# The last two expert blocks' rows enter the residual by one-hot gate products on TensorE, and the reload of the scattered rows waits for the third block from the end

## The chip, the cores and the metric

The kernel runs on one NeuronCore of a Trainium2 chip. The metric is the device time of one execution in microseconds, as a median of runs. The core has five instruction streams: PE (TensorE, matrix products), DVE (VectorE), ACT (ScalarE), POOL (GpSimd) and SP (SyncE, which issues DMAs here). They run in their own order and meet only at semaphores.

## The reference, cut to what matters

Two layers of a decoder trunk. Each is a token mixer (RWKV-7, then MoBA attention), a cross-attention and a mixture of experts; only the last matters here. 512 tokens of 1024 channels are routed to 2 of 32 experts each:

```
    y = lax.map(expert_block, (x_rows, block_expert)).reshape(n_rows, C)
    out = jnp.zeros((N, C), F32).at[row_tok].add(y.astype(F32) * row_gate[:, None])
    ...
        x = x + hierarchical_moe(h2, moe_wg[i], moe_bg[i], moe_we[i], moe_be[i],
                                 moe_w1[i], moe_w3[i], moe_w2[i]).reshape(B, T, C)
    return rms_norm(x, ln_f)
```

So each token gets two expert rows, each times its gate, added to the residual `x`. After layer 0 `x` is normed and multiplied by the query weights of MoBA (`mq`); after layer 1 it is normed and written out.

## The kernel before, in words

**Expert blocks.** The token rows are grouped into blocks of 64 rows, one expert a block, and 32 blocks ran in each layer of this execution (`E` is 32; blocks beyond `E` exist in the program behind branches, as an overflow). POOL gathers the 64 rows of a block from `h_rows` in HBM; PE turns them (`rows_in`), multiplies them by the two up matrices (`up`), turns the gated result (`turn_act`) and multiplies by the down matrix (`down`). DVE makes the gated product (`gated`), ACT copies the 128x512 result out of PSUM into `y[b]`, of which there are two, and POOL scatters it to `y_rows` in HBM by `scatter`, an indirect DMA. SP streams the expert matrices.

**The combine.** When the last block's rows have landed in `y_rows`, SP loads them back token by token: 8 DMAs of 512 KB (`combined[t]`, t = 0 to 3 tiles of 128 tokens, k = 0 and 1 the two experts of a token), in the order of t. DVE adds each, times its gate, to `x[:, t]` (`combine(t, k)`, line 1969). Then for each tile ACT takes the squares (line 857), DVE and ACT make the reciprocal root (lines 1235, 859, 1237), and DVE scales: line 1994 for layer 0, whose result PE turns (line 2413) and multiplies by the `mq` weights (line 2426), or `finished` at line 1984 for layer 1, after which SP stores the tile.

**Other loads of SP at this place.** In layer 0 the first pair of `mq` matrices (4 MB, line 499), in layer 1 the final norm's gain (`ln_f`, line 599): both stand ahead of the reload in SP's stream. SP's order is the order of the code.

**Rotary angles.** At the end of layer 0 DVE computes the angles of MoBA (lines 1953 to 1965), ahead of its first `combine`, and ACT takes two sines (lines 1074, 1075).

**PSUM banks.** `bank_group_order` is a list of names that gives each PSUM result its bank (place in the list modulo 8); `start` on PE waits until the bank's previous user is emptied, `filled` and `emptied` are the semaphores between.

## Time and profile before

| what | value |
|---|---|
| median of 3 runs | 2249.56 us (2243.38 to 2254.15) |
| profiled execution, its own time | 2244.53 us |
| span in the trace | 2242.8 us |
| TensorE granted clock, mean over the span | 0.956 of full |
| PE busy | 1941.4 us (87%) |
| DVE, ACT, POOL busy | 863.6, 453.7, 193.1 us |
| DMA moved | 511.45 MB, 228 GB/s |

The profiled execution is one run with the profiler's records; its span starts with the first instruction, so every time below is counted from there. Its own time is 1.7 us more than its span. Busy shares are means over stages with different limits; the change touches the ends of the two expert stages (about 1170 to 1211 us and 2188 to 2243 us) and a few other places.

### The profile page before, as it was taken

What the parts mean: (1) busy time and instruction counts of PE and PEld (TensorE: products, weight loads), DVE (VectorE), ACT (ScalarE), POOL (GpSimd) and SP (SyncE); (2) the same over time, 40 slices, a digit from 0 to 9 for tenths busy, and PEclk for the clock granted to TensorE, in tenths of its full rate; (3) what the DMA queues carried; (4) which work ended last, traced back from release to release, by engine and by line L of the source; (5) the groups of instructions that cost most, each with busy time, mean ns of one, the idle gap of its engine ahead of it and who ended that gap; (6) DMA issues with size and microseconds to landing.
All of it is one profiled execution on the core that took longest, in us unless ns stands there. A gap on an engine that the chain in (4) does not pass through costs nothing.

```text
span 2242.8 us, 34109 instructions
## 1 busy us (share of the span) xinstructions
PE 1941.4 (87%) x14540; PEld 1048.0 (47%) x14540; DVE 863.6 (39%) x1608; ACT 453.7 (20%) x1103; POOL 193.1 (9%) x234
## 2 busy tenths in 40 slices
PE   6999788899997888888886999999998888888783
PEld 5844777756845332332233445546845333233231
DVE  6755666684464111111013565761465111111103
ACT  2042666511111100000002005611112000000001
POOL 1000222010001111111110000000000111111110
PEclk9999999999998999999998999999998999999997
DMA  5210001413258999999994222024256999999995
GB/s 152 95 56 0 13 4 35 141 38 113 75 228 302 408 406 405 404 400 407 410 410 161 75 75 76 3 92 150 78 225 234 400 403 406 407 408 414 393 411 208
DMA packets 92181, 511.45 MB, mean 228 GB/s; under 512 B 21824, under 2 KB 22984, under 8 KB 67184
## 3 DMA queue, kind: packets, MB, share of 16 engines
q1 hardware_dynamic: 80896, 492.15, 56.4%
q0 software_dynamic: 10880, 16.81, 2.2%
q8 instruction: 130, 2.13, 0.4%
q14 instruction: 35, 0.29, 0.0%
q10 hardware_dynamic: 240, 0.07, 0.0%
HBM read 503.73 MB, written 24.12 MB: 235 GB/s over the span
## 4 chain that ended last, share of the span: by engine, by line
PE 73%; DMA 13%; DVE 8%; issue 3%; ACT 3%; ACTq 0%; POOLq 0%; SPq 0%; DVEq 0%
PE ps L2623 15%; PE ps L2081 13%; DMA big<-in_moe_w 12%; PE ps L2654 10%; PE ps L2077 9%; PE ps L2060 2%; PE ps L2273 2%; PE ps L2158 2%; PE ps L2637 1%; PE ps L2661 1%; PE ps L2426 1%; PE ps L2524 1%; PE ps L2387 1%; PE ps L2206 1%; PE ps L2536 1%
## 5 line engine op out<-in xcount | busy, mean ns | idle before, releaser
L2623 PE MATMUL ps<-big 128*64 128x512 f32 x2048 | 458.2, 600 | 1.6 <-DVE big L1925 1.6
L2654 PE MATMUL ps<-big 128*64 128x512 f32 x1024 | 269.8, 675 | 51.4 <-DMA big<-in_moe_w 28.0
L2081 PE MATMUL ps<-big 128*128 128x512 f32 x672 | 289.6, 592 | 0.0
L2623 PEld LDWEIGHTS ps<-big 128*64 128x64 f32 x2048 | 142.4, 138 | 265.1 <-issue 259.3
L1925 DVE TENSOR_TENSOR big<-ps,gain_ffn 128x512 f32<-128x512 f32 x66 | 45.6, 691 | 417.9 <-PE ps L2661 417.9
L2081 PEld LDWEIGHTS ps<-big 128*128 128x128 f32 x672 | 127.4, 190 | 159.0 <-issue 158.7
L2077 PE MATMUL ps<-big 128*128 128x256 f32 x896 | 195.6, 381 | 6.3 <-DVE big L1418 6.3
L789 POOL DMA_INDIRECT scratch<-h_rows,row_index x68 | 65.7, 967 | 1554.4 <-DVE row_index L1910 776.3
L1934 DVE SCALAR_TENSOR_TENSOR big<-big,ps 128x256 f32<-128x256 f32 x64 | 26.9, 421 | 426.7 <-ACT big L1188 426.7
L2077 PEld LDWEIGHTS ps<-big 128*128 128x128 f32 x896 | 171.2, 191 | 30.0 <-issue 6.5
L2654 PEld LDWEIGHTS ps<-big 128*64 128x64 f32 x1024 | 79.6, 153 | 193.8 <-issue 164.7
L2637 PE MATMUL ps<-ident,big 128*64 128x64 f32 x1024 | 44.3, 229 | 100.8 <-DVE big L1938 92.8
L1188 ACT ACTIVATE big<-ps 128x256 f32<-128x256 f32 x64 | 24.5, 383 | 454.3 <-PE ps L2623 454.3
L974 ACT ACTIVATE big<-ps 64x256 f32<-64x256 f32 x256 | 96.8, 378 | 63.4 <-PE ps L2273 32.3
L2637 PEld LDWEIGHTS ps<-ident,big 128*64 128x64 f32 x1024 | 35.9, 138 | 154.6 <-DVE big L1938 143.3
L1199 ACT ACTIVATE big<-ps 128x512 f32<-128x512 f32 x64 | 38.2, 597 | 323.0 <-PE ps L2654 308.6
L1303 DVE TENSOR_TENSOR big<-ps,big 128x512 f32<-128x512 f32 x112 | 70.7, 682 | 38.2 <-PE ps L2081 38.2
L796 POOL DMA_INDIRECT y_rows<-big,row_index x64 | 63.9, 998 | 60.5 <-ACT big L1199 43.5
L2273 PE MATMUL ps<-big 64*64 64x128 f32 (+1 forms) x1024 | 62.8, 262 | 2.6 <-issue 2.5
L2661 PEld LDWEIGHTS ps<-ident,scratch 64*128 64x128 f32 x528 | 37.9, 139 | 56.5 <-issue 52.0
L2158 PE MATMUL ps<-big 128*128 128x512 f32 x128 | 58.7, 617 | 4.6 <-DVE big L1437 4.6
L1337 DVE TENSOR_TENSOR big<-ps,big 128x512 f32<-128x512 f32 x64 | 41.9, 685 | 52.1 <-PE ps L2077 52.1
(347 smaller groups left out, 2403.8 us busy)
## 6 DMA issues: line engine op xcount, KB each, us to landing
big<-in_moe_w SPq DMA_DIRECT2D x182, 2048.0 KB, 30.3
big<-in_rw_wrkv SPq DMA_DIRECT2D x12, 1024.0 KB, 5.2
big<-in_mx_wkv SPq DMA_DIRECT2D x12, 1024.0 KB, 5.1
big<-in_moe_w SPq DMA_DIRECT2D x12, 1024.0 KB, 36.5
big<-in_mb_wqkv SPq DMA_DIRECT2D x12, 1024.0 KB, 6.7
big<-in_mx_wq SPq DMA_DIRECT2D x8, 1024.0 KB, 6.3
big<-in_mx_wo SPq DMA_DIRECT2D x8, 1024.0 KB, 5.0
big<-in_moe_w SPq DMA_DIRECT2D x16, 512.0 KB, 8.5
```

The source lines that it names most:

```text
L789: pool.indirect_dma_start(hg[b], None, h_rows[l], bass.IndirectOffsetOnAxis(ap=idx_rows[0:BR, n_block:n_block + 1], axis=0), bounds_check= ...
L796: pool.indirect_dma_start(y_rows[l], bass.IndirectOffsetOnAxis(ap=idx_y[:, n_block:n_block + 1], axis=0), y[b], None, bounds_check=4 * T - ...
L974: ins = A(dst[to], src[at], ACT.Copy, scale=scale)
L1303: ins = V.tensor_tensor(x[:, t, cols], bank(s + (m, i))[:], x[:, t, cols], ALU.add)
L2077: ins = mm(d[:, j * 256:(j + 1) * 256], lhsT=quarter(w)[:, k, at], rhs=acts[:, k], start=k == 0, stop=k == 3)
L2081: ins = mm(d[:], lhsT=acts[:, k, i * P:(i + 1) * P], rhs=quarter(w)[:, k], start=k == 0, stop=k == 3)
L2158: ins = mm(d[:], lhsT=tiles(RE, KT)[:, k, t * P:(t + 1) * P], rhs=w[:, k, :], start=k == 0, stop=k == KT - 1)
L2273: ins = mm(ps[4 * g + 2][r, q * P:q * P + wide.stop * L], lhsT=Y[r, q], rhs=XT[r, q, wide].rearrange("p s t -> p (s t)"), start=True, stop ...
L2623: ins = mm(ps[2 + b][half * BR:(half + 1) * BR, :], lhsT=hgT[b][:, k], rhs=w13[set_][:, :, k, half * 256:(half + 1) * 256], start=k == 0, ...
L2637: ins = mm(ps[4][r, cols], lhsT=hact[b][:, cols], rhs=ident[:, r], start=True, stop=True)
L2654: ins = mm(ps[5 + b][half * BR:(half + 1) * BR, :], lhsT=hT[b][:, f * BR:(f + 1) * BR], rhs=w2[set_][:, f, half * HB:(half + 1) * HB], sta ...
L2661: ins = nc.tensor.transpose(ps[b][:, k * BR:(k + 1) * BR], hg[b][:, k * P:(k + 1) * P], ident[at_rows, at_rows])
```

## The change

The scatters of blocks `E - 2` and up are left out (of 32 blocks: 30 and 31). Their rows stay in `y[0]` and `y[1]`. A new group of products (`late`) multiplies them on PE by a matrix that is the gate where a row of the block belongs to a token and zero elsewhere, for all four tiles, and DVE adds the result to `x`. The gates by row come from a second one-hot product beside the table's (`gates`), the matrix from 14 small DVE instructions (`late_selection`). The reload waits for the scatters up to block 29 alone, takes tile 3 first, and now stands ahead of the `mq` weights and of `ln_f` in SP's stream. Tile 3's two loaded parts are added by POOL, not by DVE. `y_rows` is zeroed once at the start by two DMAs of 4 MB. The angles move from DVE to the start of POOL's stream, the sines to ACT's stream ahead of layer 0's expert stage. POOL's descriptor scratch is halved.

```diff
-        o += attn_router_order(l) + [("rank", l), ("table", l)]
+        o += attn_router_order(l) + [("rank", l), ("table", l), ("gates", l)]
+        o += [("late", l, t, half) for t in range(TT) for half in range(2)]
...
-                if l == 0:
-
-                    sp.wait_ge(up_done[l], E - 1)
-                    load_pair(first_mix)
-                else:
-                    sp.wait_ge(up_done[l], E - 1)
-                    sp.dma_start(lnf, ln_f.partition_broadcast(P)).then_inc(lnf_loaded, 16)
...
             for j in range(2, 6, 2):
                 load_pair(j)
+            sp.wait_ge(consts, 1)
+            for l in range(2):
+                sp.dma_start(y_rows[l].rearrange("(p r) (c n) -> p (r c) n", p=P, n=256),
+                             zero[:].unsqueeze(1).to_broadcast([P, 4 * T * HB // P // 256, 256])).then_inc(y_cleared, 16)
...
                 count = experts(l)
-                sp.wait_ge(down_done[l], count)
                 for b in range(2):
-                    sp.wait_ge(y_stored[l][b], (count + (1 - b)) // 2 * 16 + 16)
-                for t in range(TT):
+                    sp.wait_ge(y_stored[l][b], (count + (1 - b)) // 2 * 16)
+                sp.wait_ge(act_ready[l], (count + 1) // 2 * 2 - 1 + PRE)
+                for t in (TT - 1, *range(TT - 1)):
                     for k in range(2):
                         sp.dma_start(combined[t][:, k * C:(k + 1) * C],
...
+                sp.wait_ge(up_done[l], E - 1)
                 if l == 0:
-
+                    load_pair(first_mix)
                     j += 2
+                else:
+                    sp.dma_start(lnf, ln_f.partition_broadcast(P)).then_inc(lnf_loaded, 16)
...
+            pool.wait_ge(pos_loaded, 16)
+            link(pool.tensor_copy(posf[:], posi[:]))
...
+                pool.wait_ge(y_cleared, 32)
...
-                    scatter(n_block)
+                    if n_block < E - 2:
+                        scatter(n_block)
...
+                for k in range(2):
+                    part = combined[TT - 1][:, k * C:(k + 1) * C]
+                    pool.wait_ge(combined_loaded[TT - 1][k], 16 * (l + 1))
+                    link(pool.tensor_scalar(part, part, gate2[:, k, TT - 1:TT], None, ALU.mult))
+                    pool.tensor_tensor(x[:, TT - 1], part, x[:, TT - 1], ALU.add).then_inc(pool_combined, 1)
+                    pool.wait_ge(pool_combined, 2 * l + k + 1)
...
+                if l == 0:
+                    A(turns_cs[:], turns_cs[:], ACT.Sin).then_inc(sines_ready, 1)
+                name = ("gates", l)
+                wait_filled(act, name)
+                A(n_blocks[:], cum[:, E - 1:E], ACT.Copy)
+                empties(A(row_gates[:], bank(name)[:, 0:NBP], ACT.Copy), name)
...
+                V.scalar_tensor_tensor(blk1g, blk1h, 0.5, bc(pairs_of(gate2[:]), [P, 2 * TT, NBP], 2), ALU.is_gt, ALU.mult
+                                       ).then_inc(gates_in, 1)
...
+                def late_selection():
+
+                    dve.wait_ge(down_done[l], E - 2)
+                    wait_emptied(dve, ("gates", l))
+                    tok, off, gates, tok_off = late_tmp
+                    link(V.tensor_copy(tok, row_index[:, 0]))
+                    link(V.tensor_scalar(off, iota_rows[:, 0:NBP], 2.0 - E, n_blocks[:], ALU.add, ALU.is_lt))
+                    link(V.scalar_tensor_tensor(tok_off, off, PAD, tok, ALU.mult, ALU.add))
+                    link(V.scalar_tensor_tensor(gates, off, 0.5, row_gates[:], ALU.is_lt, ALU.mult))
+                    for b in range(2):
+                        link(V.tensor_reduce(late_row[:, b:b + 1], tok_off[:, b::2], AX, ALU.min))
+                        link(V.tensor_reduce(late_row[:, 2 + b:3 + b], gates[:, b::2], AX, ALU.add))
+                        link(V.tensor_scalar(late_at[:, b], iota_rows[:, 0:8], -float(BR), late_row[:, b:b + 1], ALU.mult, ALU.add))
+                        link(V.tensor_tensor(late_sel[:, b], bc(iota_rows, [P, 8, BR], 1), bc(late_at[:, b], [P, 8, BR], 2),
+                                             ALU.is_equal))
+                        ins = V.tensor_scalar(late_sel[:, b], late_sel[:, b], late_row[:, 2 + b:3 + b], None, ALU.mult)
+                    ins.then_inc(sel_ready, 1)
+
                 for i, u, runs, _ in blocks(dve, count):
                     b, number = u % 2, i * UNROLL + u
+                    if isinstance(number, int) and number == E - 2:
+                        late_selection()
...
+                def late(t):
+                    if t == TT - 1:
+                        dve.wait_ge(pool_combined, 2 * l + 2)
+                    for half in range(2):
+                        name = ("late", l, t, half)
+                        wait_filled(dve, name)
+                        cols = x[:, t, half * HB:(half + 1) * HB]
+                        empties(V.tensor_tensor(cols, bank(name)[:], cols, ALU.add), name)
+                    for half in range(2):
+                        wait_emptied(dve, ("late", l, t, half))
+                    V.nop().then_inc(x_updated, 1)
...
-                combine(0, 0)
-                combine(0, 1)
+                for t in range(TT - 1):
+                    for k in range(2):
+                        combine(t, k)
+                late(0)
                 for t in range(TT):
                     if t + 1 < TT:
-                        combine(t + 1, 0)
+                        late(t + 1)
...
+                pe.wait_ge(gates_in, l + 1)
+                d = start(("gates", l))
+                for i in range(2 * TT):
+                    for half in range(2):
+                        ins = mm(d[half * BR:(half + 1) * BR, 0:NBP], lhsT=row1h[:, i], rhs=blk1g[:, i], start=i == 0,
+                                 stop=i == 2 * TT - 1)
+                finish(ins)
...
+                pe.wait_ge(sel_ready, l + 1)
+                pe.wait_ge(y_out[l], count + PRE)
+                for t in range(TT):
+                    banks = [start(("late", l, t, half)) for half in range(2)]
+                    for b in range(2):
+                        for half in range(2):
+                            r = slice(half * BR, (half + 1) * BR)
+                            ins = mm(banks[half][:], lhsT=late_sel[r, b, 2 * t:2 * t + 2], rhs=y[b][r], start=b == 0, stop=b == 1)
+                            if b == 1:
+                                finish(ins)
...
-    nc = _bacc.Bacc("TRN2", target_bir_lowering=False, num_devices=1, dynamic_dma_scratch_size=2048)
+    nc = _bacc.Bacc("TRN2", target_bir_lowering=False, num_devices=1, dynamic_dma_scratch_size=1024)
```

Where the instructions stand now. SP at the end of layer 0's expert stage, before, from the `mq` weights to the reload (the rows left out are the branches of the overflow blocks):

```order
L499 DMA big<-in_mb_wqkv 128x4x512 x4
L601 TENSOR_LOAD item_i
...
L612 UNCONDITIONAL_BRANCH
L609 REGISTER_ALU
L609 COMPARE_AND_BRANCH
L608 UNCONDITIONAL_BRANCH
L699 ISA x2
L702 DMA big<-y_rows 128x1024 x8
L499 DMA big<-in_mb_wqkv 128x4x512 x8
```

The same place of the changed kernel:

```order
L614 UNCONDITIONAL_BRANCH
L611 REGISTER_ALU
L611 COMPARE_AND_BRANCH
L610 UNCONDITIONAL_BRANCH
L704 ISA x2
L705 ISA
L708 DMA big<-y_rows 128x1024 x8
L508 DMA big<-in_mb_wqkv 128x4x512 x12
```

The four first `mq` DMAs have moved from ahead of the reload's eight to behind them.

DVE at the end of layer 0's expert stage, before: the last gated product, the angles, then the combines with the first tile's norm between them (`big<-big,gate` is `combine`, `big<-big,rstd` the norm's scaling, `big<-ps,par` an eviction of PE's transposes):

```order
L1938 SCALAR_TENSOR_TENSOR big<-big,ps 128x64x4
...
L1965 TENSOR_SCALAR scratch<-scratch 128x128
L1969 SCALAR_TENSOR_TENSOR big<-big,gate 128x1024 x3
L1235 TENSOR_SCALAR ss<-ss 128x1
L1237 RECIPROCAL rstd<-rstd 128x1
L1994 TENSOR_SCALAR big<-big,rstd 128x1024
L1969 SCALAR_TENSOR_TENSOR big<-big,gate 128x1024
L1977 TENSOR_TENSOR big<-ps,par 128x4x128
L1969 SCALAR_TENSOR_TENSOR big<-big,gate 128x1024
```

The same place of the changed kernel (`big<-ps,big 128x512` is `late`, two for each tile):

```order
L1977 SCALAR_TENSOR_TENSOR big<-big,ps 128x64x4
...
L480 UNCONDITIONAL_BRANCH
L2011 SCALAR_TENSOR_TENSOR big<-big,gate 128x1024 x6
L2021 TENSOR_TENSOR big<-ps,big 128x512 x4
L1272 TENSOR_SCALAR ss<-ss 128x1
L1274 RECIPROCAL rstd<-rstd 128x1
L2049 TENSOR_SCALAR big<-big,rstd 128x1024
L2030 TENSOR_TENSOR big<-ps,par 128x4x128
L2021 TENSOR_TENSOR big<-ps,big 128x512 x2
L1272 TENSOR_SCALAR ss<-ss 128x1
```

All six combines of tiles 0 to 2 now stand ahead of the first norm, the angles are gone, and each tile has two adds from PSUM in place of one or two combines.

PE at the same place of the changed kernel: the last turn and down product of block 31 (the rows ahead), the branches of the overflow, then the new products, before the transposes of the first normed tile:

```order
L2753 UNCONDITIONAL_BRANCH
L481 REGISTER_ALU
L481 COMPARE_AND_BRANCH
L480 UNCONDITIONAL_BRANCH
L2761 REGISTER_ALU
L2767 MATMUL ps<-big 128x512 x16
L2464 MATMUL ps<-ident,big 128x128 x8
```

The 16 products of 64x512 inputs are new; before, the transposes followed the branches.

## Rows read from the trace of the kernel before

**Rows 1.** The chain, end of layer 1: start us, us, what.

```profile
2203.38 0.43 DVE big L1934
...
2209.41 0.61 ACT big L1199
...
2210.78 3.40 DMA y_rows<-big,row_index
...
2214.57 7.21 DMA big<-y_rows
...
2221.89 1.30 DVE big L1969
...
2238.45 1.28 DVE big L1984
```

**Rows 2.** The chain, end of layer 0: start us, us, what.

```profile
1191.47 0.61 ACT big L1199
...
1203.27 1.30 DVE big L1969
...
1207.43 1.95 PE ps L2413 x8
...
1210.69 4.73 PE ps L2426 x7
```

**Rows 3.** Timeline of POOL: the scatters of block 29, layers 0 and 1.

```profile
1174.36 1.00 POOL L796 DMA_INDIRECT y_rows<-big,row_index  x1 [2.86 <-ACT big L1199]
...
2192.29 1.00 POOL L796 DMA_INDIRECT y_rows<-big,row_index  x1 [2.86 <-ACT big L1199]
```

**Rows 4.** The tile `y_rows` in 1174:1175, then 2192:2193: those scatters' landing.

```profile
DMA to landing us min/median/max: 6.5/6.5/6.5
...
DMA to landing us min/median/max: 6.7/6.7/6.7
```

**Rows 5.** DMA issues of layer 1's reload: the first, then the last.

```profile
big<-y_rows SPq DMA_DIRECT2D x1, 512.0 KB, 4.4
...
big<-y_rows SPq DMA_DIRECT2D x1, 512.0 KB, 9.4
```

**Rows 6.** The tile `y_rows`: SP's reload, first and last start.

```profile
L702 SPq DMA_DIRECT2D big<-y_rows x16: 320/720/2225, 1195.9 to 2220.8; - x16
```

**Rows 7.** Windows: PE, PEld, DVE, ACT, POOL busy, then PEclk, DMA share, GB/s.

```profile
1196.00:1197.00 1.00, 0.00 (x0) 0.00 (x0) 0.89 (x4) 0.00 (x0) 0.00 (x0) 0.82 0.23 45
...
2213.00:2214.00 1.00, 0.00 (x0) 0.00 (x0) 0.00 (x0) 0.85 (x2) 0.00 (x0) 0.90 0.09 25
```

**Rows 8.** Timeline at 444 to 460 us: DVE and POOL adding 128x1024.

```profile
444.96 1.22 DVE L1634 TENSOR_TENSOR big<-big 128x1024 f32<-128x1024 f32 x1
...
446.26 3.26 POOL L777 TENSOR_TENSOR big<-big 128x1024 f32<-128x1024 f32 x1 [61.08 <-DVE big L1634]
447.35 3.25 DVE L1634 TENSOR_TENSOR big<-big 128x1024 f32<-128x1024 f32 x1
...
459.53 2.35 POOL L777 TENSOR_TENSOR big<-big 128x1024 f32<-128x1024 f32 x1 [1.16 <-DVE big L1634]
```

**Rows 9.** Groups of PE by form: products of half height.

```profile
L2147 PE MATMUL ps<-scratch,big 64*128 64x512 f32 x32 | 7.2, 596 | 0.0
```

**Rows 10.** The page: the costliest groups, DVE's 128x512 from PSUM.

```profile
L1925 DVE TENSOR_TENSOR big<-ps,gain_ffn 128x512 f32<-128x512 f32 x66 | 45.6, 691 | 417.9 <-PE ps L2661 417.9
```

**Rows 11.** Timeline of PE, start of layer 0's expert stage.

```profile
703.05 1.14 PE L2595 MATMUL ps<-big 128*64 128x49 f32 x32 [2.13 <-DVE big L1897]
...
709.38 0.71 PE L2661 MATMUL ps<-ident,scratch 64*128 64x64 f32 x8 [1.06 <-DMA scratch<-h_rows,row_index]
```

**Rows 12.** Timeline of SP, start of the kernel.

```profile
57.85 67.11 SPq L499 DMA_DIRECT2D big<-in_rw_wrkv  x8
227.07 1.34 SPq L632 DMA_DIRECT2D scratch<-in_rw_lnx_g  x2
```

**Rows 13.** The page: DMA issues of POOL's scatters, median us to landing.

```profile
y_rows<-big,row_index POOLq DMA_INDIRECT x68, 10.2
```

More of the change, by code:

```diff
@@ L200, in trunk @@
         hid_wa, hid_g = scratch[:, 0:T], scratch[:, T:2 * T]
-        cosn, sinn = (scratch[:, i * P:(i + 1) * P].rearrange("p (t j) -> p t j", t=TT) for i in range(2))
-        ang = [scratch[:, (2 + i) * P:(3 + i) * P] for i in range(4)]
         zero = sb("zero", [P, 256])
@@ L223, in trunk @@
         row_index = sb("row_index", [P, 2, NBP], I32)
+        row_gates = sb("row_gates", [P, NBP])
+        n_blocks = sb("n_blocks", [P, 1])
+        turns_cs = sb("turns_cs", [P, 2, P])
+        cosn, sinn = (turns_cs[:, i].rearrange("p (t j) -> p t j", t=TT) for i in range(2))
         ps = [ctx.enter_context(nc.psum_tensor(f"ps{i}", [P, HB], F32)) for i in range(8)]
@@ L278, in trunk @@
         gain_loaded = sem("gain_loaded")
-        combined_loaded = [[[sem(f"combined_loaded{l}{t}{k}") for k in range(2)] for t in range(TT)] for l in range(2)]
+        combined_loaded = [[sem(f"combined_loaded{t}{k}") for k in range(2)] for t in range(TT)]
+        y_cleared, gates_in, sel_ready, pool_combined = (sem(n) for n in ("y_cleared", "gates_in", "sel_ready", "pool_combined"))
         x_updated = sem("x_updated")
@@ L406, in trunk @@
         lnf = region(4)[:, 0:C]
+        late_sel = region(1)[:, 3072:4096].rearrange("p (b j i) -> p b j i", b=2, i=BR)
+        late_tmp = [region(1)[:, 2048 + i * 64:2048 + i * 64 + NBP] for i in range(4)]
+        late_row = region(1)[:, 2304:2308]
+        late_at = region(1)[:, 2308:2324].rearrange("p (b j) -> p b j", b=2)
         combined = [R[t // 2][:, t % 2 * 2 * C:(t % 2 + 1) * 2 * C] for t in range(TT)]
@@ L755, in _ @@
                       ).then_inc(consts, 1)
+            pool.wait_ge(pos_loaded, 16)
+            link(pool.tensor_copy(posf[:], posi[:]))
+            a0, a1 = (turns_cs[:, 1 - i] for i in range(2))
+            g3 = lambda a: a.rearrange("p (t j) -> p t j", t=TT)
+            link(pool.tensor_tensor(g3(a0), posf[:].unsqueeze(2).to_broadcast([P, TT, 32]),
+                                    inv_freq[:].unsqueeze(1).to_broadcast([P, TT, 32]), ALU.mult))
+            link(pool.tensor_scalar(a1, a0, 1 / (2 * math.pi), ROUND_MAGIC, ALU.mult, ALU.add))
+            link(pool.tensor_scalar(a1, a1, ROUND_MAGIC, None, ALU.subtract))
+            turns = scratch[:, 0:P]
+            for part in TWO_PI_PARTS:
+                link(pool.tensor_scalar(turns, a1, -part, None, ALU.mult))
+                link(pool.tensor_tensor(a0, a0, turns, ALU.add))
+            link(pool.tensor_scalar(a0, a0, PI_BELOW, -PI_BELOW, ALU.min, ALU.max))
+            link(pool.tensor_scalar(a1, a0, 0.0, -2.0, ALU.min, ALU.mult))
+            link(pool.tensor_tensor(a1, a1, a0, ALU.add))
+            pool.tensor_scalar(a1, a1, -1.0, math.pi / 2, ALU.mult, ALU.add).then_inc(angles_ready, 1)
             wait_filled(pool, ("bonus",))
@@ L814, in _ @@
                         gather(first)
-                        scatter(first - 2)
+                        scatter(first - 4)
                         for n_block in range(first + 1, min(first + 5, NBP)):
@@ L818, in _ @@
                                 gather(n_block)
-                                scatter(n_block - 2)
+                                scatter(n_block - 4)
+                for k in range(2):
[4 more added lines that the diff above has]
+                    pool.wait_ge(pool_combined, 2 * l + k + 1)
                 pool.wait_ge(gathers_ended, l + 1)
@@ L841, in wait_x @@
                 elif norm == 3:
[L842 removed]
+                    act.wait_ge(x_updated, t + 1)
                 elif norm == 4:
@@ L895, in _ @@
             wait_filled(act, ("hidden_wa",))
+            act.wait_ge(angles_ready, 1)
             A(hid_wa[0:64, :], bank(("hidden_wa",))[0:64, :], ACT.Tanh)
@@ L1072, in _ @@
                 if l == 1:
-                    act.wait_ge(angles_ready, 1)
-                    A(sinn, ang[0].rearrange("p (t j) -> p t j", t=TT), ACT.Sin)
-                    A(cosn, ang[1].rearrange("p (t j) -> p t j", t=TT), ACT.Sin).then_inc(sines_ready, 1)
                     A(gst[0:1, 1:2], ones[0:1, 0:1], ACT.Sqrt)
@@ L1967, in combine @@
-                def combine(t, k):
-                    dve.wait_ge(combined_loaded[l][t][k], 16)
-                    V.scalar_tensor_tensor(x[:, t], combined[t][:, k * C:(k + 1) * C], gate2[:, k, t:t + 1], x[:, t],
-                                           ALU.mult, ALU.add).then_inc(x_updated, 1)
-                    dve.wait_ge(x_updated, 8 * l + 2 * t + k + 1)
+                def combine(t, k):
+                    dve.wait_ge(combined_loaded[t][k], 16 * (l + 1))
+                    link(V.scalar_tensor_tensor(x[:, t], combined[t][:, k * C:(k + 1) * C], gate2[:, k, t:t + 1], x[:, t],
+                                                ALU.mult, ALU.add))
@@ L1994, in _ @@
                         V.tensor_scalar(XN[:, t], x[:, t], rstd[:, t:t + 1], None, ALU.mult).then_inc(xn_ready, 1)
-                        if t + 1 < TT:
-                            combine(t + 1, 1)
                         mix_turned(t)
@@ L1999, in _ @@
                         finished(t)
-                        if t + 1 < TT:
-                            combine(t + 1, 1)
         @block.tensor
```

23 lines of the change are left out of this document (4 added, 19 removed).

## Prediction

> **What bounds the kernel now.** I read the chain of waits first, over the ends of the two expert stages. The reader is to see in layer 1's [rows 1] one thread without slack. Block 31's result is copied out until 2210.0 (2209.41 + 0.61); its scatter takes from 2210.78 to 2214.2; then the reload, in which the second DMA lands at 2221.8 (2214.57 + 7.21); only then comes the second combine, to 2223.2. So 13.2 us pass between the last copy and the moment when tile 0 of `x` is complete, and no engine computes on the chain but for 1.3 of them. From there the four tiles' norms run to the last scaling's end at 2239.7 (2238.45 + 1.28), and the last store ends the span at 2242.8, 3.1 later. Layer 0 is alike [rows 2]: the copy ends at 1192.1, tile 0 is complete at 1204.6 (1203.27 + 1.30), PE's transposes start at 1207.4 and its first `mq` product at 1210.7. After that PE goes on from product to product, so what layer 0 gains is what that start gains.
>
> Next I looked at when a reload that waits for block 29 alone may start. Its scatter is issued at 1174.4 and 2192.3 [rows 3] and lands 6.5 and 6.7 us later [rows 4]: 1180.9 and 2199.0. Before, the reload started at 1195.9 and 2214.2 [rows 1, 6]. It starts 15.0 and 15.2 us earlier. That isn't the gain, because a reload takes long: its first DMA lands after 4.4 us, its last, issued at 2220.8, after 9.4 [rows 5, 6], which is 2230.2, or **16.0 us after the start** for all eight. Before, the first combine needed one DMA of the eight and tile 0 two; the rest ran beside the norms. Now `late(0)` stands behind six combines, that need all eight.
>
> **The change part by part, layer 1.**
>
> *The reload.* Start 2199.0. First landing +4.4, second +7.6, the other six evenly to +16.0 (1.4 each): tile 3's parts at 2203.4 and 2206.6, then tile 0 at 2208.0 and 2209.4, tile 1 at 2210.8 and 2212.2, tile 2 at 2213.6 and 2215.0. DVE has its last gated product behind it (it starts it at 2203.38, rows 1) and would end the sixth combine at 2215.0 + 1.3 = 2216.3, if it ran free.
>
> *It does not run free.* POOL now scales and adds tile 3's parts, four instructions of 128x1024, from 2203.4 on. What two such engines do to each other is in the trace [rows 8]: DVE's add of two SBUF tiles takes 1.22 us by itself and 3.25 beside POOL's add. It starts at 447.35, ends at 450.6, and POOL had begun at 446.26. POOL's takes 3.26 there and 2.35 where DVE has only copies from PSUM. The combine too reads two SBUF tiles. The Trainium skill, "SBUF — State Buffer", section "Who interferes with whom", says that a DVE instruction with two SBUF inputs and a GpSimd one that reads SBUF exclude each other for the whole instruction; by that rule, too, the combines wait, and it speaks against giving tile 3 to POOL; without it the sum would be the unblocked one, which is a rival below.
> So I let the two take turns. POOL's add is 2.3 (2.35, rows 8). Its scaling of 128x1024 has no row; it reads half as much, so I take 1.5, between nothing and 2.35. (The Trainium skill, "GPSIMD Engine Reference", section "3.1 Elementwise", gives 1.8 cycles an element at 1.2 GHz as a tight loop's rate; an estimate from it for 1024 is 1.5 as well.) POOL: scaling to 2205.0, add to 2207.4, scaling to 2209.0. Combine 1 asks at 2208.0, runs 2209.0 to 2210.3; POOL's last add to 2212.6; combines 2 to 6 one after another, 1.3 each, end at **2219.1**. With 2.35 for the scaling POOL gets its last add only after combine 2, and the six end at 2220.6. Unblocked 2216.3.
>
> *The late products.* PE may start when y(31) is copied, 2210.0, and its branches are done. The nearest row is 16 products (32 records) of 64 rows by 512 in 7.2 us [rows 9], with alternating halves of the array as here. 2210.1 + 7.2 = 2217.3 for all, 2211.9 for tile 0: ahead of DVE, so nothing. One after another at 0.86 each it would be 3.4 a tile, 2213.5 and then 2223.9 for the last, still ahead of DVE's need (2220.5 and 2226, below). The 14 instructions of `late_selection` cost at most 14 x 0.69 = 9.7 us [rows 10], and DVE is free for them from about 2192.3 to 2203.38: hidden. Were they longer, they would delay block 31's gated product and with it PE, which has 7 us before tile 0's adds.
>
> *Tile by tile.* `late(0)` is two adds of 0.69 [rows 10] and a wait for their end, 1.5 together: tile 0 complete at 2220.6, where it was 2223.2: **2.6 us gained**. Then the order helps. Before, squares, root, scaling and the next combine stood in one row. From tile 0 complete to the last scaling's start were 15.3 us (2238.45 - 2223.2): three times a scaling and a combine (2.5), and four times squares and root, which leaves 1.9 each; squares of 1024 columns are about as long as a combine, 1.3, so the root's small steps are 0.65. Now the next tile is complete while this one's root is made, its squares too, and DVE's own work sets the pace: adds 1.5, small steps 0.65, scaling 1.3 = 3.45; the last has no adds behind it and waits for its squares, 1.9. From tile 0 complete to the last scaling's end: 2.15 + 2 x 3.45 + 1.9 + 1.28 = 12.2, where it was 2239.7 - 2223.2 = 16.5. **4.3 us gained.** Layer 1: 6.9. With the slow scaling 5.4, unblocked 9.7. The `ln_f` load, now behind the reload, has from 2215 to the first scaling at 2222.8; the eighth reload DMA needs 9.4 in a full queue, so it is covered, barely.
>
> **Layer 0.** The same 18.1 us earlier (1180.9 for 2199.0): combines end at 1201.0, tile 0 complete at 1202.5, where it was 1204.6: 2.1. `late(1)` stands ahead of tile 0's mean, 0.2 more than the squares take, so the transposes start at 1205.5 and not 1207.4. PE's clock: granted 0.82 in the mean of the us from 1196 on and 0.90 from 2213 on [rows 7], so it fell from 2.4 to 1.2 GHz about 5.2 and 4.4 us after the last product (1191.4, 2209.3). The late products end at 1199.5, the transposes come 6 us later, so they find it low as before; 1.95 us, then the same 1.3 to the first `mq` product: 1208.8 for 1210.7. **1.9 us gained.** The `mq` weights: all reload data are there at 1197, three of the four DMAs of 1 MB that the first product needs come behind. At the reload's own pace (4 MB in 16 us, its latency in it) that is 12 us, 1209; faster, it is hidden. The angles leave DVE, which waited for the reload there: nothing. With slow scaling the start gains 0.4.
>
> **Start of the expert stages.** The gates' product is like the table's, 1.14 us [rows 11], ahead of PE's fill-in products; PE then waits 1.06 for the gathered rows. 0.1 each, up to 0.3 with ACT's copy: 0.2 in all.
> **Start of the kernel.** The zeroing (8.4 MB) is issued at 125.0 (57.85 + 67.11) and SP has nothing until 227.07 [rows 12]; 82 GB/s are enough, and the reload got 262. Nothing. POOL's angles: it idles there. Nothing.
>
> **The sum.** 6.9 + 1.9 - 0.2 = 8.6 us. The profiled execution (span 2242.8, 2244.5 by its own time) would be 2234.2 in span. Its own time was 5 us below the median of the runs shown; from the median, 2249.6 - 8.6 = **2241.0 us**. Bounds: 5.4 + 0.4 - 0.6 = 5.2 us at least if nothing else waits; at most 9.7 + 6.5 (second rival) - 0.2 = 16.
>
> **The rivals.** *The forecast*, DVE and POOL in turns and a low clock at the `mq` start: 6 to 11 us, chance 0.47.
> *More than 11 us*, 0.35. Either the combines aren't blocked (2216.3), against which rows 8 speak, or PE's clock stays up in layer 0, for which there is little missing: if the late products take longer than 7.2 us, the transposes come less than 5 us behind them. Then the transposes take half of 1.95, and the first seven `mq` records, 4.73 [rows 2], take 3.2 at the 0.45 a record of rows 9's pairs (7.2 / 16): 2.5 more, 11.1. Both together: tile 0 at 1199.8, first `mq` product at 1205.5 to 1206, 6.5 for layer 0, 16 in all, 2233.
> *Hidden or given back*, 0 to 5 us, 0.12. The late products run singly and at the low clock (27 us): tile 3's come at 2238, and `late(3)`, which wants them at 2227, waits 10 us in layer 1. Or `mq` weights or `ln_f` come some us late.
> *Slower*, 0.06. One mechanism: POOL's halved descriptor scratch no longer holds the descriptors of several indirect DMAs, so POOL waits for a landing before each issue. A scatter lands after 10.2 us in the busy stage [rows 13], a gather not much sooner; two in turn are about 20, and a block takes 15 (32 blocks from 709.4 to 1191.5, rows 2 and 11). 5 us x 60 blocks is 300 us, 2540. It decides only if fewer than two DMAs fit in the half; no row shows how many do, and the changed program issues none more often than before.
>
> **How the numbers follow.** The range reaches from the unblocked end (2233) less 2 for the runs' scatter to no change: 2231 to 2249. Within 0.5% (11 us, about what a measurement of this kernel can tell from no change) is the forecast and most of the third: 0.57; faster 0.37; slower 0.06.
>
> **What would show it.** The reload's first DMA starts within 0.5 us of 1181 and 2199, and all eight land 16 us later. DVE's combines measure more than 1.28 where POOL works, and POOL's adds 3 us and more. Tile 0 complete at 2220 to 2221. Scalings 3.4 apart. PE's late products end before DVE's adds of their tile. The clock column at the transposes of layer 0 says 0.50. I am wrong if POOL's gathers are late in the expert stage, if the combines stay at 1.28, or if the reload takes other than 16 us now that it starts beside the last blocks.

## The result, and the profile after

The changed kernel takes **2252.59 us** (median of 20 runs, 2245.63 to 2690.9; all but the highest lie under 2260, and that one ran at a granted clock of 0.83 where the others have 0.96), the kernel before 2247.41 (20 runs on the same chips, 2241.03 to 2254.15). The ratio is 1.0022, 95% interval 1.0012 to 1.0033. The forecast was 2241.0, with 2231 to 2249 as its range. The profiled execution took 2248.42 by its own time.

From the page of the changed kernel: its span, the engines' busy time, the DMA packets that brought instructions (packets, MB, share), and POOL's scatters:

```profile
span 2246.6 us, 34441 instructions
...
PE 1955.6 (87%) x14668; PEld 1053.4 (47%) x14668; DVE 885.0 (39%) x1639; ACT 455.1 (20%) x1107; POOL 219.8 (10%) x252
...
q8 instruction: 131, 2.15, 0.4%
...
L822 POOL DMA_INDIRECT y_rows<-big,row_index x60 | 59.9, 999 | 25.4 <-issue 17.1
```

The chain at the end of layer 1, which answers to [rows 1] (start us, us, what):

```profile
2214.96 0.61 ACT big L1236
2215.57 10.89 issue
2226.46 5.48 PE ps L2767 x16
2231.94 1.28 DVE big L2021 x2
...
2242.28 1.28 DVE big L2037
```

In [rows 1] DMAs stood between the last copy and tile 0. They are gone from here, as was intended. In their place stand 10.89 us of "issue", time in which PE waited for nothing that this view shows, and then the late products (line 2767). Layer 0, which answers to [rows 2], is worse:

```profile
1187.33 0.60 ACT big L1236
1187.93 16.24 issue
1204.17 9.73 PE ps L2767 x32
1213.89 1.04 PE ps L2464 x8
1214.93 0.02 issue
1214.95 1.15 ACT big L1114 x4
1216.10 0.14 issue
1216.24 4.10 PE ps L2477 x9
```

The first `mq` product starts 28.3 us after the last copy's end, where it was 18.6 [rows 2]. In layer 1 the last scaling ends 28.0 us after the copy, where it was 29.7 [rows 1]. Loss 9.7, gain 1.7; of the loss 1.5 come back, because ten `mq` products now take 4.53 us at the full clock, where PE's timeline of before has them at 6.02. 9.7 - 1.5 - 1.7 is 6.5 us, and the medians differ by 5.2. So these two places account for the result. (In the profiled execution the last copy of layer 0 also ended 4.2 us earlier than before. Over the thirteen kernels profiled here it ends anywhere between 1185.9 and 1196.0 us, so I don't ascribe that to the change.) What is left to explain is what PE did between the last down product and the first late one.

What the other engines did meanwhile is shown by the timeline of DVE, POOL and SP in layer 1 (start us, us, engine and line, the operation, then the idle time ahead of it and what ended it):

```profile
2205.00 3.93 SPq L708 DMA_DIRECT2D big<-y_rows  x8
2208.97 0.47 SPq L716 DMA_DIRECT2D big<-in_ln_f  x1
2210.58 2.84 POOL L851 TENSOR_SCALAR big<-big,gate 128x1024 f32<-128x1024 f32 x1 [11.74 <-DMA big<-y_rows]
2213.50 2.35 POOL L852 TENSOR_TENSOR big<-big 128x1024 f32<-128x1024 f32 x1
2214.48 11.75 DVE L2011 SCALAR_TENSOR_TENSOR big<-big,gate 128x1024 f32<-128x1024 f32 x6 [4.50 <-DMA big<-y_rows]
2215.95 3.69 POOL L851 TENSOR_SCALAR big<-big,gate 128x1024 f32<-128x1024 f32 x1
2219.73 2.78 POOL L852 TENSOR_TENSOR big<-big 128x1024 f32<-128x1024 f32 x1
2230.28 1.29 DVE L2021 TENSOR_TENSOR big<-ps,big 128x512 f32<-128x512 f32 x2 [4.04 <-PE ps L2767]
...
2233.97 1.28 DVE L2037 SCALAR_TENSOR_TENSOR big<-big,rstd 128x1024 f32<-128x1024 f32 x1
...
2237.22 1.28 DVE L2037 SCALAR_TENSOR_TENSOR big<-big,rstd 128x1024 f32<-128x1024 f32 x1
```

The combines end at 2226.2, 10.7 us after the copy, and DVE then waits 4.04 us for PE. The scalings follow each other in 3.25 us, as forecast (3.45).

PE's own branch records, which the profile's views leave out because they count as no work, say where the "issue" comes from. This is an ordinary list made from the trace: for each layer the copy's end and every record of a branch on PE over 0.3 us (start, duration; the other six or so take 0.21 each; the first ones come before the copy, since PE's sequencer runs ahead of its products).

```
before layer 0: copy ends 1192.07 | 1187.87 0.37; 1188.58 3.12; 1192.58 2.29; 1195.53 4.32
before layer 1: copy ends 2210.00 | 2205.80 0.35; 2206.77 2.76; 2210.39 2.64; 2213.36 4.44
after  layer 0: copy ends 1187.92 | 1184.03 0.35; 1185.26 4.99; 1190.85 5.40; 1196.31 7.60
after  layer 1: copy ends 2215.56 | 2211.36 0.36; 2212.61 5.44; 2218.64 2.62; 2221.65 4.54
```

These are the conditions around the blocks past the 32nd, none of which runs here: blocks 32 to 35 are written out, each with its conditions, and a loop stands behind them (`blocks`). PE takes ten branches over them. In both kernels three are long, one after the other. Before, they ended 7.8 us after the copy, and PE wasn't wanted for another 7.6 in layer 0 and not at all in layer 1. Now the late products stand right behind them, and they end 16.0 and 10.6 us after the copy.

The trace also has the packets of the instruction queue (16 KB each), and each long branch has one or two of them. The time from the branch's start to its first packet's start tells the wait in the queue from the fetch itself. In layer 0 of the changed kernel, while 380 to 418 GB/s of reload and weights move, it is 2.6, 2.8 and 3.4 us. In layer 1 it is 3.1 us for the first branch, beside 363 to 412 GB/s, and 0.2 and 0.4 for the other two, when the reload has landed. Before, it is at most 0.4 us in both layers.

### The profile page after: what moved, and what is told of

The parts are those of the page before. It is cut to its first block, busy times and chain, and to the rows that moved or that the text cites. A ratio compares the mean times of both kernels' runs of the same rounds, so it can differ in the third digit from the quotient of the medians.

```text
span 2246.6 us, 34441 instructions
## 1 busy us (share of the span) xinstructions
PE 1955.6 (87%) x14668; PEld 1053.4 (47%) x14668; DVE 885.0 (39%) x1639; ACT 455.1 (20%) x1107; POOL 219.8 (10%) x252
## 4 chain that ended last, share of the span: by engine, by line
PE 73%; DMA 12%; DVE 8%; issue 4%; ACT 3%; ACTq 0%; DVEq 0%; POOLq 0%
PE ps L2681 14%; PE ps L2132 12%; DMA big<-in_moe_w 12%; PE ps L2712 10%; PE ps L2128 9%; PE ps L2111 2%; PE ps L2324 2%; PE ps L2209 2%; PE ps L2695 1%; PE ps L2719 1%; PE ps L2575 1%; PE ps L2257 1%; PE ps L2587 1%; PE ps L2477 1%; PE ps L2098 1%
```

## The experiments

Theory A at the outset: a taken branch to code that PE doesn't hold makes it wait for instructions, and those are fetched by DMA behind the reload and the weights. Rivals: PE waits for the value of `count` or for `y_out`, or the late products wait for something of DVE's or POOL's.

**The overflow code away**, in both kernels and in PE's stream alone; PE then leaves out blocks past the 32nd, which these inputs don't have.

```
                     with runs(number):
                         turn_act(b, number)
                         down(b, set_, number, turn, i * (UNROLL // 2) + (u // 2 + 1))
+                    if isinstance(number, int) and number == E - 1:
+                        break
```

> The changed kernel without the code of the overflow blocks (32 and up) in PE's stream alone; they never run here, so the result is the same. Theory A: PE starts the late products 17 us (layer 0) and 12 us (layer 1) after its last down product because the branches over that code leave it without instructions, and the fetch of the next ones queues behind the reload and the mq weights. Then PE starts them within 1.5 us of the copy of y(31), tile 0 is complete some 10 us earlier in layer 0 and 4 us earlier in layer 1, and the kernel takes about 12 to 15 us less than the changed one. Theory B: PE waits for data or a semaphore there (the selection, the copied y, a bank) that the trace doesn't name: the gap stays at 17 and 12 us and the time at that of the changed kernel.

> The kernel before with the same code taken out of PE's stream, as the control. Theory A: in layer 0 PE's next instructions are wanted only when tile 0 is normed, 15 us after the last product, and in layer 1 never, so the fetch is hidden: within 2 us of the kernel before. If it gains several us, then the fetch was a cost before too, and part of what the first kernel gains is not the change's.

**PE's overflow code as a short loop** of two blocks, which still computes them where there are any.

```
+                    if isinstance(number, int) and number == E - 1:
+                        with runs(number + 1):
+                            rows_in(b)
+                            up(1 - b, set_1, number + 1, turn_1, range(KT))
+                        break
...
+                with pe.If(count > E):
+                    with pe.Fori(0, (NB - E + 1) // 2) as i:
+                        for u in range(2):
...
```

> The changed kernel with PE's overflow blocks as one compact loop of two blocks instead of four blocks written out and a loop of twelve; it handles every count as before. Theory A: the jump goes over some 150 instructions instead of 1,500, so that the target is in or next to what PE holds; PE's gap shrinks to under 6 us, and the kernel is 8 to 15 us faster than the changed one, thus 3 to 10 us faster than before. If any taken branch costs the fetch, whatever its distance, the gap stays. Theory B: the gap stays at 17 and 12 us.

**A small reload**: 16 of each row's 1024 columns are reloaded, so that the kernel leaves out the rest of these rows, its results are not the reference's, and only the traffic is gone.

```
-                        sp.dma_start(combined[t][:, k * C:(k + 1) * C],
+                        sp.dma_start(combined[t][:, k * C:k * C + 16],
```

> The changed kernel whose eight reload DMAs take 16 of 1024 columns each; the rest of the expert rows isn't added, the instructions are the same. Theory A: the fetch waits in the DMA queues behind data, so in layer 1, where nothing else is in them, PE's gap falls from 12 us to 3 to 5 us; in layer 0 the 4 MB of mq weights now follow at once, and the gap stays at 10 us or more. If the fetch just takes long by itself, both gaps stay. Theory B: both stay.

Measured, with the second group of runs. The ratio is to the kernel before, run in between on the same chip. The four columns behind it are worked out from each profiled execution: us from the end of the last copy of `y` to the start of the late products (PE) and of the first `mq` product in layer 0, and to the late products' start and the last scaling's end in layer 1. The groups ran on different chips, on which the kernel before took 2248.29 us (the first four), 2250.40 (the two with one padded condition, before_short_skip and short_tile3_dve) and 2250.65 (the last three), so across groups the ratios are safer than the medians.

```
kernel                 median us  ratio (95%)             L0 late  mq    L1 late  end
before                 2247.41                              -      18.6    -      29.7
changed                2252.59    1.0022 (1.0012-1.0033)    16.2   28.3   10.9    28.0
late_no_overflow       2231.91    0.9932 (0.9913-0.9952)     0.1   16.4    0.1    21.6
before_no_overflow     2239.42    0.9963 (0.9951-0.9976)    -      16.3    -      27.4
late_short_skip        2233.83    0.9937 (0.9918-0.9956)     0.1   16.4    1.2    22.3
late_small_reload      2245.68    (one run)                 12.7   24.6    6.8    23.9
late_pad_200           2236.37    0.9940 (0.9925-0.9956)     0.1   13.3    2.2    23.7
late_pad_1500          2236.55    0.9934 (0.9919-0.9949)     1.9   18.0    2.4    23.5
late_pad_8x188         2292.17    1.0172 (1.0149-1.0194)    32.9   45.2   29.0    46.9
late_one_branch        2240.05    0.9941 (0.9920-0.9962)     0.1   13.5    4.4    23.7
before_short_skip      2240.29    0.9955 (0.9941-0.9969)    -      16.4    -      27.6
short_tile3_dve        2224.32    0.9896 (0.9879-0.9914)     0.1   12.8    1.5    18.5
short_mq_first         2247.08    0.9976 (0.9961-0.9992)     0.1   28.0    0.1    20.7
```

Without the code over which PE jumped, nothing else touched on PE, the late products start as soon as the copy is done. PE's timeline, layer 1, without the overflow code:

```profile
2203.74 7.14 PE L2769 MATMUL ps<-big 64*128 64x512 f32 x32 [0.76 <-ACT big L1236]
```

The waits for the selection and for `y_out` against `count` are the same there, so these rivals fall. With PE's code made short instead of left out nearly the same comes out (0.1 and 1.2 us). Both gain more than was expected, 20.7 and 18.8 us under the changed kernel for 12 to 15 and 8 to 15; and the kernel before gains too, 9 us for an expected 2 at most, so part of that gain isn't the change's (more on this below). The small reload shortens the gap in layer 1 from 10.9 to 6.8 us (expected 3 to 5): about 4 of it are the queue behind the reload, the rest a price of the branches by themselves. Before's list says the same: branches end 7.8 us after the copy, in layer 1 beside at most 200 GB/s.

**Amount of code or number of jumps?** Never executed matmuls stand ahead of the late products in the kernel without overflow code: 100 or 750, each with its weight load, under one condition, and then 8 times 94.

```
+                with pe.If(count > NB - 1):
+                    for _ in range(750):
+                        mm(ps[0][0:BR, 0:BR], lhsT=ident[:, 0:BR], rhs=ident[:, 0:BR], start=True, stop=True)
```

> The kernel without the unexecuted overflow blocks, with 750 matmuls and their 750 weight loads, never executed, under one condition ahead of PE's wait for the late products. Theory A (a taken branch over much code leaves PE without instructions until they are fetched): the late products again start 7 to 17 us after y(31) is copied, where they started 0.05 us after it without the code, and the time is 2239 to 2248 us. Rival (what the removed code cost lies in the other engines, or in what PE executed, not in PE's distance): the products start at once and the time stays at 2232 us.

> The same with 100 matmuls and 100 weight loads, never executed. Theory A (the price is of the distance): the branch's target is nearly or already fetched, so the products start at most 2 us after the copy and the time is 2231 to 2235 us. Rival (the price is of the branch, whatever its distance): as with 1,500 instructions, 2239 us or more.

> The kernel without the overflow blocks, with the same 1,500 never executed instructions as in the run with one condition over them (2236.6 us, products 1.9 and 2.4 us after the copy), here under eight conditions one behind the other, each over 94 matmuls and 94 weight loads. Theory D: several long branches in series, the products start 6 to 16 us after the copy, 2242 to 2252 us. If only the distance counts: as with one condition, 2235 to 2238 us.

Theory A was wrong in its form. 1,500 instructions under one branch take the time of 200 in the medians, 2236.55 and 2236.37, between what A and its rivals had for either; the products start 1.9 and 2.4 us after the copy with 1,500 (A had 7 to 17), 0.1 and 2.2 with 200. Under eight branches the same 1,500 cost 55.6 us more, 2292.17 for 2236.55 (some 54 by the ratios). That is the direction of theory D, each jump for itself, but far more than its 2242 to 2252 us and its 6 to 16 us to the products. PE's timeline in layer 0, eight branches:

```profile
1189.12 3.65 PE L2712 MATMUL ps<-big 128*64 128x512 f32 x16 [0.48 <-ACT big L1232]
1226.33 9.97 PE L2773 MATMUL ps<-big 64*128 64x512 f32 x32 [33.55 <-issue]
```

Its branch records, list made from the trace as above:

```
late_pad_1500  layer 1: copy ends 2211.66 | 2207.46 6.36
late_pad_8x188 layer 1: copy ends 2242.43 | 2237.38 5.92; 2243.36 3.45; 2246.87 4.80; 2251.73 3.21;
                                            2255.01 4.89; 2259.96 2.95; 2262.97 4.98; 2268.00 3.15
```

And the pages count the packets that brought instructions (packets, MB, share), with one condition and with eight:

```profile
q8 instruction: 125, 2.05, 0.4%
```

```profile
q8 instruction: 145, 2.38, 0.5%
```

Twenty packets of 16 KB more, ten in each layer, for the same code. All eight jumps of layer 1 and seven of layer 0 are long, 3 to 5 us each in quiet queues and 6 to 7 beside the transfers, and each record starts when the one before it has ended. So theory D took A's place: **the price is per jump, in series**. It isn't the price of every jump: the first of the eight in layer 0 took 0.36 us, so did the one over 200 instructions in layer 0 (the one over 1,500 took 5.87 there), and of the ten over the overflow code seven are short. Which jump finds its target ready stays open. The Trainium skill, "Runtime: NRT & Kernel Launch", section "Instruction fetch mechanics", says that a taken branch whose target lies outside what the instruction memory holds forces a DMA fetch before the engine goes on; the traces agree, by these packets and by the branch records.

**One condition around all of PE's overflow blocks**, written out as before.

```
-            for u in range(UNROLL):
+            over = eng is nc.tensor
+            for u in range(E - sure // UNROLL * UNROLL if over else UNROLL):
                 yield sure // UNROLL, u, some, False
             first = sure // UNROLL + 1
+            if over:
+                with eng.If(count > E):
+                    for u in range(E - sure // UNROLL * UNROLL, UNROLL):
+                        yield sure // UNROLL, u, some, False
+                    with eng.If(count > UNROLL * first):
...
```

> The changed kernel with PE's overflow blocks as written out as before, and one condition (count over 32) around all of them, so that PE jumps twice where it jumped ten times over the same code. Theory D (each jump to code that is not yet there costs a fetch, one after the other: 5.0, 5.4 and 7.6 us of branch records in layer 0, 5.4, 2.6 and 4.5 in layer 1): at most two long branches, of which the first starts before y(31) is copied, so the late products start 2 to 6 us after the copy and the time is 2234 to 2241 us. Theory A in its first form (the price is of the amount of code jumped over): as in the changed kernel, products 11 to 16 us after the copy and 2250 us or more.

12.5 us less than the changed kernel in the medians and 18 by the ratios (0.9941 for 1.0022), with the same code in place and two jumps for ten. One long record is left (5.89 us in layer 0, started 6.4 us before the copy's end, and 7.89 in layer 1), and the products start 0.1 and 4.4 us after the copy, sooner than D's 2 to 6 in layer 0 and within it in layer 1.

**The control: the short loop in the kernel before.**

> The kernel before, with PE's overflow blocks as one compact loop of two in place of the written-out ones, the other engines as they were: the control for the changed kernel with the same edit (2233.8 us). Theory A: in the kernel before PE has 16 us to fetch in, so the edit gives it nothing there: 2244 to 2248 us, and the change with a short skip is worth 10 to 14 us. Rival (PE's code length costs elsewhere in both kernels, through the traffic of its fetches): 2239 to 2241 us, as without any overflow code, and the change is worth 6 us.

The rival was right: it is 10 us faster, as without any overflow code. Part of it is seen. With ten jumps SP's eight reload DMAs take 6.5 and 7.7 us to issue; the records of DMA issue of layer 0 in the kernel before are up to 1.50 and 1.24 us long where 0.43 is the rule. With the short loop they take 4.0 and 4.4. Along with that go 2.2 us in each layer (16.4 for 18.6, 27.6 for 29.7). That the fetches are the cause is not shown: the changed kernel with the short skip takes 6.8 us for the same eight in layer 0, with no long jump beside them. The other 5 to 6 us I did not find; the profiled executions differ by 1.8 only and stages bound by DMA vary by as much. So the change with the short skip is to be held against this control, not against before alone: 0.9937 to 0.9955 of before, intervals that overlap, so a gain isn't shown there. In the kernels without overflow code it is 0.9932 to 0.9963, 7.5 us in the medians.

**Tile 3's combines on DVE** instead of POOL, on top of the short skip. The reload is then issued in the order of the tiles, where it had tile 3 first.

```
-                for t in (TT - 1, *range(TT - 1)):
+                for t in range(TT):
...
-                for k in range(2):
-                    part = combined[TT - 1][:, k * C:(k + 1) * C]
...
-                for t in range(TT - 1):
+                for t in range(TT):
                     for k in range(2):
                         combine(t, k)
```

> The changed kernel with PE's short skip, and tile 3's two combines moved from POOL to DVE behind those of the other tiles, with the reload in the order of the tiles. If the turns with POOL cost what its share saves (combines took 11.5 us for six where DVE alone takes 1.3 each): DVE's eight end 8 to 9 us after y(31) is copied as its six did, and the time is 2232 to 2235 us. If POOL's share shortens the path: two combines more, 2236 to 2238 us. If the turns cost more than it saves: 2229 to 2231 us.

It is the best kernel of all, 1.0% under before, and faster than all three cases expected. Timelines of DVE in layer 0, for the short skip with POOL's share and for this kernel:

```profile
1185.17 10.59 DVE L2011 SCALAR_TENSOR_TENSOR big<-big,gate 128x1024 f32<-128x1024 f32 x6 [5.36 <-DMA big<-y_rows]
```

```profile
1182.88 10.53 DVE L2005 SCALAR_TENSOR_TENSOR big<-big,gate 128x1024 f32<-128x1024 f32 x8 [0.93 <-issue]
```

And DVE's timeline with the small reload and POOL's share, layer 1, where the rows are there before DVE asks for them:

```profile
2210.93 11.27 DVE L2011 SCALAR_TENSOR_TENSOR big<-big,gate 128x1024 f32<-128x1024 f32 x6 [0.90 <-issue]
```

Eight combines alone take 10.5 us, 1.31 each (11.3 in layer 1, where they wait for rows now and then). Six beside POOL take 10.6 and 11.5 in the short skip, and 12.2 and 11.3 in the small reload with their rows waiting. So POOL's two cost DVE at least as much as DVE would need to do them itself; its share saved nothing. But the length of the combines isn't what this edit gained. Their start is: the first combine comes 6.1 and 5.3 us after the reload's first DMA is issued, where it came 10.7 and 9.1 us after it while POOL's tile stood first in the reload. The last one ends 5.9 and 5.0 us after the copy, where it was 8.7 and 9.2. How much of that the order of the reload would give with POOL's share kept was not run.

The rest is the clock. PE's timeline of layer 0, transposes and first `mq` products, short skip and then tile 3 on DVE:

```profile
1200.17 1.94 PE L2464 MATMUL ps<-ident,big 128*128 128x128 f32 x8 [4.58 <-DVE big L2049]
1203.44 7.33 PE L2477 MATMUL ps<-big 128*128 128x512 f32 x10 [1.32 <-ACT big L1114]
```

```profile
1197.83 1.07 PE L2456 MATMUL ps<-ident,big 128*128 128x128 f32 x8 [0.85 <-DVE big L2041]
1200.32 4.53 PE L2469 MATMUL ps<-big 128*128 128x512 f32 x10 [1.43 <-ACT big L1108]
```

And a window of each during the `mq` products (us, then busy time of PE, PEld, DVE, ACT and POOL, the granted clock, the DMA share, GB/s):

```profile
1204.00:1206.00 2.00, 2.00 (x3) 0.67 (x2) 1.07 (x3) 0.53 (x3) 0.00 (x0) 0.50 0.00 0
```

```profile
1200.00:1202.00 2.00, 1.68 (x4) 0.87 (x5) 0.94 (x4) 1.31 (x4) 0.00 (x0) 1.00 0.31 110
```

PE waits 4.58 us for DVE ahead of the transposes in the first, and its clock is at 1.2 GHz when they come; 0.85 us in the second, and it stays at 2.4. 3.6 (start of `mq`) + 2.8 (clock) + 3.8 (end of layer 1) = 10.2 us, and the medians differ by 9.5.

**The loads of `mq` weights and of `ln_f` ahead of the reload**, as before, on top of the short skip.

> The changed kernel with PE's short skip (2233.8 us), and the loads of layer 1's first weights and of ln_f issued ahead of the reload, as in the kernel before. If their place behind the reload is worth something: the reload's rows land 2 to 5 us later, the six combines end that much later, and the time is 2236 to 2241 us. If the reload's wait for block 29's scatter hides them: 2232 to 2235 us.

13 us lost in the medians and 9 by the ratios, more than either case. It lies in layer 0, where the first `mq` product starts 11.6 us later; layer 1 ends 1.6 us earlier. SP's timeline, layer 0:

```profile
1168.20 14.79 SPq L508 DMA_DIRECT2D big<-in_mb_wqkv  x2
1184.59 6.06 SPq L713 DMA_DIRECT2D big<-y_rows  x8
```

SP needs 14.8 us to issue the last two of the four `mq` DMAs, so the reload starts only 6 us before the copy's end, and the weights' own transfer lies ahead of it. The combines start 7.8 us after the copy, `mq` 28.0. The kernel before has the same long issues (11.4 and 2.6 us), but there the reload waits for block 31's scatter in any case.

## Why the prediction was wrong, step by step

- **The step that failed** is the late products': "PE may start when y(31) is copied, 2210.0, and its branches are done [...] ahead of DVE, so nothing". The branches were named and given no price. They end 16.0 and 10.6 us after the copy. DVE was done with its combines at 9.8 and 10.7 and then waited for PE, 10.3 us in layer 0 and 4.0 in layer 1. Part of the price stood in the branch records of before: with their end 7.8 us after the copy, tile 0's two products (1.8 of the 7.2) would have been ready at 9.6, where the sum has DVE ready at 9.1. The rest is that the fetches of layer 0 and the first of layer 1 now wait 2.6 to 3.4 us in queues full of reload and weights (at most 0.4 before), and that PE's clock is down to 0.50 when they end: the products take 9.7 and 8.9 us and not 7.2. I had read PE's idle time there as time that nobody wanted, and didn't ask what it was made of.
- **Without that step the sum held.** In the kernels without overflow code the change gives 7.5 us in the medians (2239.42 to 2231.91); forecast 8.6. Layer 1 gives 5.8 there (27.4 to 21.6; forecast 6.9), layer 0 nothing (16.3 and 16.4; forecast 1.9). The changed side is where the sum put it: the first `mq` product 16.4 us after the copy for a forecast 16.7, the last scaling's end 21.6 for 22.8. What the sum didn't have is that the kernel before gets 2.3 us faster at each place by losing that code. The two places give 5.7 us of the 7.5; the rest is not located.
- **The reload** went about as forecast. It starts 9.8 and 10.6 us ahead of the copy's end (forecast 11.2 and 11.0). The forecast's own sign, a start within 0.5 us of 1181 and 2199, is missed (1178.1 and 2205.0), mostly because the copies themselves end 4.2 us earlier and 5.6 later than before. The landings of its eight DMAs in layer 1 are below; the last was issued at 2208.5, so all are there at most 15.7 us after the start at 2205.0 (forecast 16.0).

```profile
DMA to landing us min/median/max: 5.5/9.7/12.2
```

- **DVE and POOL in turns**: right in kind, six combines take 12.4 and 11.8 us where 7.8 would do. The price of POOL's scaling was too low: 2.85 us for a forecast 1.5, above the 2.35 that I had held for its bound. Yet from POOL's first scaling to the last combine's end are 15.7 us in both layers, what the sum had (2203.4 to 2219.1) with 1.5 and not with 2.35 (17.2): a right length from a wrong price, luck in part, since the real turns fell otherwise than I had laid them. DVE's end came 10.7 us after the copy and not 9.1 because layer 1's reload started 0.4 us later against the copy and its first rows landed after 5.5 us and not 4.4. The turns should have been read as a reason to doubt the split: with tile 3 on DVE and the reload in the tiles' order 9.5 us go, where my rival "unblocked" had 2.8.
- The tiles follow each other as forecast (3.25 for 3.45, the last 1.8 for 1.9). The start of the expert stage costs nothing that can be seen (layer 0: 6.33 us from the table's product to the first turned rows in both kernels), nor do the zeroing and the angles; the halved scratch neither (scatters 999 ns each, as before).
- The clock at layer 0's transposes was full and not 0.50, since the products came late, just ahead of them. The rival "clock stays up" happened for a reason that cost more than it gave.
- The range ended at 2249, no change. Its upper side held only waits whose rows I had, and the one unpriced item on PE was not among them.

## What to carry to other kernels

Before work is put on an engine behind a stretch where it seemed idle, ask what it did there: branches over unused code can fill it, and the records of branches, not the busy time, show it. Price jumps by their number, up to one fetch of 2 to 8 us each and in series, and put one condition around everything that seldom runs, first on the engine that is about to be waited for. When two engines hold each other up, giving one of them part of the other's work can save nothing; weigh the helper's operations by a row of the same kind, and look whose rows the shared transfer brings first.

## What the runs showed of the hardware

- A jump over 188 never executed instructions took 3.0 to 5.0 us while at most 15 GB/s moved and 5.9 to 7.3 beside 358 to 410 GB/s. One over 200 took 6.1 and one over 1,500 6.4 us in layer 1 beside the reload, but 0.36 and 5.87 in layer 0. After eight in series the products started 29 and 33 us after the copy.
- Instruction fetches wait behind bulk DMA: from a long branch's start to its first packet at most 0.4 us before, 2.6 to 3.4 beside reload and weights. PE's long branches were 2.3 to 4.4 us before and up to 7.6 there. The other way round isn't shown: SP's issue of the reload took 6.5 and 7.7 us beside ten jumps and 4.0 and 4.4 beside two, but 6.8 and 6.1 in layer 0 of two kernels with no long jump beside it.
- POOL's multiplication of 128x1024 by a value per partition takes 2.85 us, longer than its addition of two such tiles (2.35), and 3.7 beside DVE.
- Six of DVE's combines beside two scalings and two additions of POOL take 10.6 to 12.4 us in the changed kernel, the short skip and the small reload, eight of them alone 10.5 and 11.3.
